# A two-block transformer kernel: RWKV state kept block-diagonal, MLP fed before its norm's root, attention bias masked in halves

## What is computed

```python
# first block, neighbourhood attention: relative position bias, keys outside the window masked
s = q @ k.T * scale + bias
s = where(col_valid, s, -inf);  p = softmax(s);  o = p @ v

# second block, RWKV-7, 16 heads of 64; state S is 64x64 per head, advanced token by token
y_c = groupnorm(rwkv7_recurrence(r, decay, k, v, kk, a)) * g + b + bonus

# second block, its MLP
x = x + m @ w_out[l]
h2 = rms_norm_2(x, norm2_g[l])          # x * rsqrt(mean(x*x) + eps) * gain
x = x + jnp.square(jax.nn.relu(h2 @ mlp_w1[l])) @ mlp_w2[l]
return rms_norm_2(x, final_g)
```

## Time and profile before

| | us |
|---|---|
| median of 3 runs (2917.3 to 2920.46) | 2918.0 |
| the profiled execution's own time | 2919.07 |
| span of its profile | 2917.3 |
| TensorE matmuls busy | 2867.0 |
| VectorE / ScalarE / GpSimd busy | 1538.2 / 683.4 / 1659.5 |

### The profile page before, as it was taken

The page is one execution under the profiler, slowest core; times in us unless marked ns, Lnnn a source line. Parts: engine busy times, 40 slices in busy tenths (PEclk is TensorE's granted clock), DMA queues, the critical chain, the costliest instruction groups (busy, mean ns, idle before and its releaser), DMA issues.

```text
span 2917.3 us, 44880 instructions
## 1 busy us (share of the span) xinstructions
PE 2867.0 (98%) x18304; PEld 2253.9 (77%) x18304; DVE 1538.2 (53%) x2276; ACT 683.4 (23%) x1163; POOL 1659.5 (57%) x1340
## 2 busy tenths in 40 slices
PE   8999999999999999999999999999999999999998
PEld 6766787888877767778888777777777777788886
DVE  7888876555225674453332384565465456372342
ACT  2444212000013442111000133233323333210000
POOL 6434577887765234577767744344434434566764
PEclk9999999999999999999999999999999999999999
DMA  9323553443333112232223321112112212223221
GB/s 308 126 92 131 191 170 109 151 158 133 134 94 88 35 60 69 68 115 94 94 97 105 99 65 62 54 63 68 49 61 68 69 47 72 76 87 101 94 96 63
DMA packets 102373, 285.52 MB, mean 98 GB/s; under 512 B 26030, under 2 KB 37038, under 8 KB 101934
## 3 DMA queue, kind: packets, MB, share of 16 engines
q1 hardware_dynamic: 85280, 274.68, 27.8%
q10 hardware_dynamic: 16910, 8.28, 1.4%
HBM read 280.76 MB, written 6.06 MB: 98 GB/s over the span
## 4 chain that ended last, share of the span: by engine, by line
PE 89%; DVE 7%; issue 1%; ACT 1%; DMA 1%; SPq 0%; ACTq 0%; DVEq 0%; POOL 0%; POOLq 0%
PE ps L338 25%; PE ps L339 23%; PE ps L340 23%; PE ps L1314 3%; PE ps L1134 3%; PE ps L1144 2%; PE ps L1154 2%; DVE first_mod L1629 1%; PE ps L1359 1%; DVE work L1594 1%; PE ps L1456 1%; PE ps L970 1%; DVE hR L1601 1%; PE ps L1436 0%; DVE mg L1714 0%
## 5 line engine op out<-in xcount | busy, mean ns | idle before, releaser
L561 POOL TENSOR_TENSOR wR<-raw,wR 128x512 fp32r<-128x512 f32 (+1 forms) x866 | 1189.6, 1392 | 37.6
L557 POOL CAST wR<-raw 128x1024 fp32r<-128x1024 f32 (+4 forms) x470 | 476.0, 1013 | 1189.0 <-PE ps L340 1054.8
L338 PE MATMUL ps<-hR,wR 128*128 128x512 f32 x2224 | 902.3, 406 | 10.7 <-DVE hR L1650 10.7
L339 PE MATMUL ps<-hR,wR 128*128 128x512 f32 x2224 | 870.4, 391 | 0.0
L340 PE MATMUL ps<-hR,wR 128*128 128x512 f32 x2224 | 869.9, 391 | 0.0
L338 PEld LDWEIGHTS ps<-hR,wR 128*128 128x128 f32 x2224 | 419.3, 189 | 118.1 <-issue 21.3
L340 PEld LDWEIGHTS ps<-hR,wR 128*128 128x128 f32 x2224 | 419.1, 188 | 90.0
L339 PEld LDWEIGHTS ps<-hR,wR 128*128 128x128 f32 x2224 | 419.8, 189 | 83.1 <-issue 4.8
L338 PE MATMUL ps<-act_f,wR 128*128 128x512 f32 x352 | 137.8, 391 | 0.0
L1608 DVE SCALAR_TENSOR_TENSOR xT<-ps,lm,xT 128x512 f32<-128x512 f32 x32 | 24.0, 751 | 215.5 <-PE ps L340 215.4
L340 PE MATMUL ps<-act_f,wR 128*128 128x512 f32 x352 | 137.0, 389 | 0.0
(11 more groups left out here) (373 smaller groups left out, 4171.4 us busy)
## 6 DMA issues: line engine op xcount, KB each, us to landing
raw<-in_weights_dram SPq DMA_DIRECT2D x468, 512.0 KB, 3.3
first_mod<-in_weights_dram SPq DMA_DIRECT2D x16, 512.0 KB, 10.0
raw<-in_weights_dram SPq DMA_DIRECT2D x50, 128.0 KB, 2.4
raw<-in_weights_dram SPq DMA_DIRECT2D x16, 256.0 KB, 3.0
bias_copies<-bias_rows ACTq DMA_DIRECT2D x2, 1905.0 KB, 10.1
bias<-bias_copies ACTq DMA_DIRECT2D x16, 224.0 KB, 6.0
raw<-in_weights_dram SPq DMA_DIRECT2D x8, 384.0 KB, 10.6
xT<-in_x_dram SPq DMA_DIRECT2D x1, 2048.0 KB, 9.4
```

Of the source, the lines that this page charges most:

```text
L338: mm(out, w_hi, r_hi, start=first, stop=False)
L339: mm(out, w_hi, r_lo, start=False, stop=False)
L557: nc.gpsimd.tensor_copy(wR[:, u, 0, 0:cols], raw[:, r % RING, 0:cols]).then_inc(hi_done, 1)
L561: ins = nc.gpsimd.tensor_tensor(wR[:, u, 1, part], raw[:, r % RING, part], wR[:, u, 0, part], ALU.subtract)
```

## The change

The state gets 128 columns: each head's 64x64 block stands on its own partitions and columns, and the rest is set to zero once per channel tile by two memsets. The two-head pairs L1445 and L1451 become one whole-array matmul each, u goes into one bank. The values' part of y (L1448) moves behind the wait for u. The fill steps are dealt out anew: 2 in each chunk, then 2 and 5. VectorE writes the new state in two instructions, one for each head, and scales 128 columns of the old one.

Ahead of the second block's MLP the inputs are x times the gain, without the root. ScalarE makes square and high part of each tile as soon as its residual is done, VectorE the low part. The sum over channels of the squares is one matmul in the middle of the first pair of products, and `rs` becomes the root's inverse squared (Exp with scale -1.0). It is multiplied in behind the down products, in `scaled_residual`. `keep_busy` and the two-part sum go.

The bias is masked in two instructions of two heads each, the first where the whole stood, the second in step 1 of the attention; each waits for its own four DMAs.

```diff
@@ block.scalar
-                                      ...).then_inc(s_bias, 16)
+                                      ...).then_inc(s_bias[h // 2], 16)
...
-                    A(us[:], ps[:, 2:4, 0:64], ACT.Copy).then_inc(u_sb, 1)
+                    A(us.rearrange("p h n -> p (h n)"), ps[:, 2, 0:P], ACT.Copy).then_inc(u_sb, 1)
...
-            norm(Count(Q1), Count(R1), Count(P_OUT2))
-            round_h(H0 + KD, 0)
+            for k in range(KD):
+                if k == KD - 1:
+                    log_and_exp()
+                evacuated(act, Count(P_OUT2 + k))
+                square(xT[:, k, :], Count(Q1 + k))
+                A(hR[:, 0, k, :], xT[:, k, :], ACT.Copy, scale=gs[:, 1, k:k + 1]).then_inc(h_rounded, 1)
+            act.wait_ge(mlp_summed, 1)
+            A(rt, ps[:, SUM, :], ACT.Ln, bias=epsb[:, 0:1], scale=1.0 / D).then_inc(log_ready, 1)
+            logs.append(R1)
+            act.wait_ge(log_ready, len(logs))
+            act.wait_ge(root_used, R1 + 1)
+            A(rs, rt, ACT.Exp, scale=-1.0).then_inc(root_ready, 1)
@@ block.tensor, the chain
                 def u_of_v(cc, last):
                     for h in range(2):
-                        mm = MM(ps[:, 2 + h, 0:64], mats["MT"][:, h, cc, :], ..., start=True, stop=last)
+                        mm = MM(ps[:, 2, 64 * h:64 * h + 64], mats["MT"][:, h, cc, :], ...,
+                                start=(h == 0), stop=last and h == 1)
...
                     if cc:
                         pe.wait_ge(st_sb, 3 * m + cc)
-                        for h in range(2):
-                            mm = MM(ps[:, 2 + h, 0:64], kkB[half_of(h), cols], old[half_of(h), :], start=False, stop=True)
-                        mm.then_inc(u_psum, 1)
-                    for h in range(2):
-                        MM(ps[half_of(h), 5, cols], vtok[:, cc, half_of(h)], mats["GK"][:, h, cc, :], start=True, stop=False)
-                    if cc:
-                        for h in range(2):
-                            MM(ps[half_of(h), 5, cols], old[half_of(h), :], rB[half_of(h), cols], start=False, stop=False)
-                    if not cc:
-                        fill(1)
+                        MM(ps[:, 2, 0:P], kkB[:, cols], old, start=False, stop=True).then_inc(u_psum, 1)
+                        MM(ps[:, 5, cols], old, rB[:, cols], start=True, stop=False)
+                    fill(1)
                     pe.wait_ge(u_sb, CH * m + cc + 1)
...
                     if cc < CH - 1:
                         u_of_v(cc + 1, False)
+                    else:
+                        fill(1)
+                    for h in range(2):
+                        MM(ps[half_of(h), 5, cols], vtok[:, cc, half_of(h)], mats["GK"][:, h, cc, :], start=(cc == 0), stop=False)
+                    if cc < CH - 1:
                         for h in range(2):
                             MM(ps[half_of(h), 6, 0:64], ktok[:, cc, half_of(h)], vtok[:, cc, half_of(h)], start=True, stop=False)
-                    else:
-                        fill(1)
...
-                        fill((1, 2, 1)[cc])
+                        fill(1)
                 mm.then_inc(y_psum, 1)
-                fill(3)
+                fill(2)
                 pe.wait_ge(y_sb, m + 1)
                 MM(ps[:, 6, :], blk[:], yB[:], start=True, stop=True).then_inc(mean_ready, 1)
-                fill(6)
+                fill(5)
@@ block.tensor, ahead of the MLP
-                merge_steps(u, slot, bank, range(KD - 1))
-                if u == KD - 1:
-                    first_sums(R1, 2 * DEPTH + 1)
-                merge_steps(u, slot, bank, range(KD - 1, KD)).then_inc(tile_used, 1)
-            last_sums(Count(Q1))
-            keep_busy()
+                merge_steps(u, slot, bank, range(KD)).then_inc(tile_used, 1)
+
+            def sum_of_merged():
+                pe.wait_ge(root_used, R1 + 1)
+                pe.wait_ge(acc_ready, 2 * DEPTH + 1)
+                MM(ps[:, SUM, :], ones[:], tmp, start=True, stop=True).then_inc(mlp_summed, 1)
             for hh in range(2):
-                pair_of_products((G_MLP + 32 * hh, G_MLP + 32 * hh + 1), H0 + KD)
+                pair_of_products((G_MLP + 32 * hh, G_MLP + 32 * hh + 1), H0 + KD, None if hh else sum_of_merged)
@@ block.vector, mask and state
-                dve.wait_ge(s_bias, 128 * l + 128)
-                v(V.tensor_tensor(bv, bv, colmask[:].unsqueeze(1).broadcast_to([P, 56, GRID]), ALU.add))
+                def mask_bias(pair):
+                    dve.wait_ge(s_bias[pair], 64 * l + 64)
+                    v(V.tensor_tensor(bv, bv, colmask[:].unsqueeze(1).broadcast_to([P, 28, GRID]), ALU.add))
+                mask_bias(0)
...
+                    if s == 1:
+                        mask_bias(1)
...
+                        v(V.memset(state[0:64, :, 64:P], 0.0))
+                        v(V.memset(state[64:P, :, 0:64], 0.0))
...
-                    if cc:
-                        STT(new, ps[:, 6, 0:64], f, olds[:], ALU.mult, ALU.add).then_inc(st_sb, 1)
-                    else:
-                        TS(new, ps[:, 6, 0:64], f, None, ALU.mult).then_inc(st_sb, 1)
+                    for h in range(2):
+                        rows_, at = slice(64 * h, 64 * h + 64), slice(64 * h, 64 * h + 64)
+                        if cc:
+                            ins = STT(new[rows_, at], ps[rows_, 6, 0:64], f[rows_], olds[rows_, at], ALU.mult, ALU.add)
+                        else:
+                            ins = TS(new[rows_, at], ps[rows_, 6, 0:64], f[rows_], None, ALU.mult)
+                        if h:
+                            ins.then_inc(st_sb, 1)
+                        else:
+                            v(ins)
@@ block.vector, ahead of the MLP and behind it
                 plain_residual(Count(G_OUT2 + u), Count(P_OUT2 + u), u)
-                if u < KD - 1:
-                    add_square(Count(Q1), u)
-            for k in range(KD):
-                evacuated(dve, Count(P_OUT2 + k))
-            take_root(Count(R1))
-            norm(H0 + KD, 1, 0)
+                evacuated(dve, Count(P_OUT2 + u))
+                add_square(Count(Q1), u, KD - 1)
+                dve.wait_ge(h_rounded, H0 + KD + u + 1)
+                STT(hR[:, 1, u, :], xT[:, u, :], gs[:, 1, u:u + 1], hR[:, 0, u, :], ALU.mult, ALU.subtract).then_inc(h_ready, 1)
...
+            def scaled_residual(t, p, m_):
+                dve.wait_ge(tile_used, (t + 1).value())
+                v(TT(hf, ps[:, ACC + p.mod(2), :], rs, ALU.mult))
+                v.sync()
+                TT(xT[:, m_, :], hf, xT[:, m_, :], ALU.add).then_inc(bank_free[p.mod(2)], 1)
...
+                if hh == 0:
+                    take_root(Count(R1))
+                    dve.sem_inc(root_used, 1)
                 for u in range(KD):
-                    plain_residual(Count(G_MLP + 17 + 2 * u + 32 * hh), Count(P_MLP + 16 + u + 24 * hh), u)
+                    scaled_residual(Count(G_MLP + 17 + 2 * u + 32 * hh), Count(P_MLP + 16 + u + 24 * hh), u)
```

More of the change, by code:

```diff
@@ L438, in build @@
                                     for b in (lt[:], tt[:, 1], tt[:, 0]))
-                us, sas, state, olds = xx[:, 0, 0:2, :], xx[:, 0, 2:4, :], xx[:, 1, 0:2, :], xx[:, 1, 2, :]
+                us, sas = xx[:, 0, 0:2, :], xx[:, 0, 2:4, :]
+                state = xx[:, 1].rearrange("p (b h) n -> p b (h n)", b=2)
+                olds = off[:, 0, 0:2, :].rearrange("p h n -> p (h n)")
         with ExitStack() as r:
@@ L461, in build @@
         s_pad = sem("s_pad")
-        s_bias = sem("s_bias")
+        s_bias = [sem(f"s_bias{i}") for i in range(2)]
         raw_ready = [sem(f"raw_ready{i}") for i in range(RING)]
@@ L472, in build @@
         sq_ready, sq_used = sem("sq_ready"), sem("sq_used")
-        root_ready, root_used, log_ready, gain_squared = (
-            sem(n) for n in ("root_ready", "root_used", "log_ready", "gain_squared"))
+        root_ready, root_used, log_ready, gain_squared, mlp_summed = (
+            sem(n) for n in ("root_ready", "root_used", "log_ready", "gain_squared", "mlp_summed"))
         h_ready, full_ready, h_rounded = sem("h_ready"), sem("full_ready"), sem("h_rounded")
@@ L587, in load_bias @@
                         act.dma_start(bias[64 * half:64 * half + 64, h],
-                                      bass.AP(dram_copies, first, [[BIAS_ROWS - 1, GRID], [127, 14], [1, GRID]])).then_inc(s_bias, 16)
+                                      bass.AP(dram_copies, first, [[BIAS_ROWS - 1, GRID], [127, 14], [1, GRID]])).then_inc(s_bias[h // 2], 16)
             act.wait_ge(s_x, 16)
@@ L955, in h_lo, with pair_of_products @@
                 return hR[:, 1, k, :]
-            def pair_of_products(ts, H):
+            def pair_of_products(ts, H, after_half=None):
                 slots, banks = {}, (PAIR, PAIR + 1)
@@ L972, in pair_of_products @@
                             mm.then_inc(tile_used, 1)
+                    if k == KD // 2 - 1 and after_half:
+                        after_half()
```

(7 more changed lines are left out.)

9 lines of the change are left out of this document (5 added, 4 removed).

## The result

| | before | after |
|---|---|---|
| median, us (runs) | 2918.35 (2917.3 to 2920.46, 4) | 2893.59 (2891.24 to 2895.29, 4) |
| ratio to before, 95% interval | | 0.9914 (0.9897 to 0.9931) |
| the profiled execution's own time | 2919.07 | 2892.69 |
| span of its profile | 2917.3 | 2890.9 |

The change takes off 24.8 us by the medians; the forecast was 17.8. Between the two profiled spans the difference is 26.4.

A forecast was written before the change was run, and what follows sets the result against it. TensorE, busy 98% of the span, bounds the kernel; -11.0 - 6.6 + 0.75 - 0.9 = -17.8 takes 2919.07 to 2901.3, or 2900 us against the median. Range 2896 to 2905 (chance 0.62), wider 2893.5 to 2908 (0.80).

The forecast's parts named there:

- Part 1: The chain: 1.20 us removed and 0.79 added per chunk, 0.41 saved on 24 chunks, plus first chunks: -11.0 us.
- rival A: The chain's 0.37s are issue time of small float32 groups behind a wait, not drains; no gain there, 2911; chance 0.12.
- (a): Chain, u's copy on ScalarE: ends 0.77 behind the u matmuls' start, covered by y and a step, some 1.2.
- (d): Chain, scaling the old state on VectorE: some 0.3 for 128 columns, ends before L1467 behind `conv_in`, costed at nothing.
- (c): Chain, new state's handoff: VectorE done at 0.96 behind L1467's start, TensorE needs it at 1.22; margin 0.26.
- Part 2: The MLP norm: the 6.62 us lost ahead of the second block's pair of products goes, -6.6 us; bounds -4 and -7.
- Part 3: Scaled residuals: a second VectorE instruction each, only the last on the path at the kernel's end, +0.75 us; bound 1.7.
- Part 4: The mask in layer 0: the 0.93 stall in step 1's score group goes, -0.9 us; bounds 0 and -1.1.
- B: In the chain, tiling pays and whole-array matmuls cost more: 1.55 added against 1.20, 2919.5 in all; chance 0.05.
- C: At the state's handoff, the new state comes late at u and slows the kernel; at 1.3 late, 2925; chance 0.03.
- D: The norm's gap partly becomes a wait for the sum, or handoff stalls eat chain gain: about 2907; chance 0.10.
- E: In the chain, L1448 nearly free where it now stands, drains longer than counted: 17 gained there, 2894; chance 0.08.

The follow-up runs named there:

- e1: The kernel before with only the chain change (block-diagonal state, fill steps dealt out anew): 2900.72 us, ratio 0.9941.
- e5: The kernel after with the values' part of y (L1471) back between the whole-array groups: 2905.3 us, +11.7 against after.
- e4: The kernel after with the state's part of y again as two 64x64 matmuls: 2901.22 us, +7.6 against after.
- e8: The kernel after with one more VectorE instruction, writing an unread buffer, ahead of the new state's signal: 2900.15 us, +6.5 against after.
- e6: The kernel after with `conv_in` on VectorE one chunk later, behind the state of chunk 1: 2893.0 us, ratio 0.9908 to the kernel before.
- e3: The kernel before with only the mask split into two halves: 2915.51 us, ratio 0.9993 (0.9983 to 1.0002).
- e9: The kernel after with tile 0's LRU decay rate moved earlier, to the wait for the first triangular blocks: 2892.53 us, ratio 0.9912 to the kernel before.

## Why the prediction was right or wrong

**What bounds** stood: TensorE's stream, and 24.8 us out of it.

**Part 1 failed, in the sum "0.79 added against 1.20 removed".** I forecast 0.41 a chunk; the chunk of the earlier trace rows, with two steps on either side, went from 4.34 to 3.69, by 0.65. By the steps of that sum:
- u 0.22 (0.23 taken). L1471 0.27 (0.25 taken; the worry about its place was right, and its size too).
- y 0.14, not 0.23: its successor, a matmul of the same tile shape, starts 0.14 behind it. 0.09 too much was counted.
- Restart 0.09 at the step behind y (0.08 taken), entry 0.09 removed, as taken.
- Not counted at all: a change of shape also lengthens what lies behind it. The factor's group took 0.49 behind 64*64 tiles and takes 0.39 behind a step (in the first chunk of before, where it stood behind a step too, it took 0.38); the first 128*64 group took 0.17 behind whole-array tiles and takes 0.11 behind another of its shape. 0.16 together.

0.41 + 0.09 + 0.10 + 0.06 - 0.02 = 0.64. In a tile's first chunk the same omission was larger in proportion: 0.41 (4.10 to 3.69) instead of 0.15, since L1436 took 0.48 ahead of other tiles and L1450 0.36 ahead of its own shape (0.12), and the entry of u (0.09) and the 0.06 come on top. The stretches from a tile's first L1450 to its three u and to L1487 were 4.10, 4.33, 3.63 and 5.00 and are 3.70, 3.69, 3.70 and 4.45; the third has a step of 0.68 more. That is 2.2 a tile, where the whole tile measured 2.19, 17.5 for eight. e1 shows it for the part alone; e5 and e4 each put one visit back and show 0.35 for it.

I read the drain from the distance of the changed group to its successor, 0.37, and that was right; the same rows, 2479.61 to 2480.10 and 2480.64 to 2480.81 against 2480.81 to 2480.92, held the remainder. I even used 0.49 and 0.17 in rival A as evidence and took them for plain work. The bound of 15 to 16 that I gave for part 1 lacked them too.

**Its cover.** (a) and (b) held: no wait of TensorE is released by u's or sa's copy. (d) held in its cost only: the scaling ends 0.46 behind the start of L1478 (2462.39 + 0.29), where I had it end ahead of it. (c) held in its result only. VectorE begins 0.49 behind L1478 here, not 0.40, since the scaling of 128 columns and `conv_in` are in front (0.41 in the next chunk, without them), its two halves take 0.60, not 0.56, and the weights of u must be there before u. Margin: 0.07 at most, not 0.26 (e8), with no cost yet (e6). That was luck and not cover.

**Part 2 held**: 6.55 for 6.6, the pair with its sum 2539.32 - 2527.54 = 11.78 for 11.8. The sum's matmul starts at 2532.98 and the running sum was done at 2530.80, a margin of 2.2 for the 2 I gave. One step was off without effect: the low part takes 1.54 to 1.67 in seven of eight tiles, not 0.8. It too reads two operands from SBUF beside GpSimd's work, as the running sum does (0.69 with GpSimd idle, 0.93 to 1.71 beside it); the loop takes 0.69 + 1.60 + 1.67 = 3.96, for the 3.9 I had as the most, under the 5.4 of a product.

**Part 3 held**: 0.72 for 0.75. **Part 4 held** against this execution of before, 1.05 for 0.9 by the trace, and with luck: the stall that I priced is in two of the three profiles without the edit (e3).

Sum against the profiled execution: 2919.07 - 17.8 was 2901.3, measured 2892.69, so 8.6 more. Part 1's 6.5, the clock's 1.55 that only this execution of before had, 0.4 of small shifts and 0.15 of the mask are those 8.6. Against the medians only part 1 and the small ones are left, since the runs of before hold some without the dip.

**Rivals.** A falls: part 1 gave more than the forecast, and the same group cost 0.27 among its kind, and 0.37 with 0.18 in front of it elsewhere (e5). B falls with e4. C didn't come, by a margin thinner than thought (e8). D falls: no wait for the sum, and the waits at the handoff cost nothing (e6). E had the size, 17 for part 1, and half the reason: the drains were longer than counted, but L1448 was no more free than I took it to be. I gave it a chance of 0.08, having looked only for the cost of entering a shape.

## What to carry to other kernels

Price a change of tile shape at both its ends: add up the whole stretch from a group well ahead to one well behind it, and compare it with a stretch of one shape. Here work with a visit took 0.35 us longer than the same work without one, so a whole-array matmul with half its operand zero beat two exact small tiles, and groups of one shape belong side by side. A factor common to a whole column of a product can wait until behind it; what stood in front of TensorE (6.6 us) then costs one vector instruction at the very end (0.72).

## What the runs showed of the hardware

- A pair of float32 matmuls on 128*64 tiles costs 0.35 us more between whole-array matmuls than among its own kind (e5: a chunk of 4.04 against 3.69), and a pair on 64*64 tiles 0.35 more than the one whole-array matmul that does its work (e4: the same 4.04).
- Two whole-array float32 matmuls of 128 columns in a row start 0.22 apart, but a step of 512 columns starts 0.14 behind the second, with 0.09 given back at the next start.
- A weight load may be 0.2 late for VectorE without TensorE losing anything (3.69 with, 3.68 to 3.69 without); an instruction of 0.23 more in front of it costs 0.19 to 0.35 (e8).
- A running sum of 128x512 float32 with both operands in SBUF takes VectorE 0.69 us with GpSimd idle and 0.93 to 1.71 beside its work (L1630 in after).
- Behind one and the same wait of some 2 us the granted clock stood at 0.50 in some executions (before, e6, e8) and at 1.00 in others (after and seven experiments); it was worth 1.55 us. It moves elsewhere too: at the last matmul with ones it cost 0.94 in e9. A profile of one execution carries it into every difference, so line up two traces event by event before a term is put down to an edit.
